# Seven quarter products in place of one: product 5 of the channel groups, with one buffer for x's two sets of combinations

## The reference, cut to what matters

```python
h = rmsnorm(x, norm_g)
proj = h @ w_in                       # 1024 -> 12288 channels
b_a, c_a, x_a, z_a, q, k, v, z_b, g_a, g_b = split(proj)
u = conv3(c_a * x_a) + conv_b         # causal, depthwise
y_a = (b_a * u * silu(z_a)) @ w_a_out
q, k = rotary(q), rotary(k)
o = retention(q, k, v)                # 4 heads, chunks of 128
y_b = (rms(o) * silu(z_b)) @ w_b_out
x = x + (sigmoid(g_a) * y_a + sigmoid(g_b) * y_b) @ w_o
out = rmsnorm(x, final_g)
```

## Time and profile before

| | |
|---|---|
| median of the runs | 1368.4 us |
| the profiled execution's span | 1366.5 us |
| around the span, by these two | 1.9 us |
| TensorE busy | 1354.6 us, 99% |
| VectorE busy | 1063.1 us, 78% |
| ScalarE busy | 591.4 us, 43% |
| GpSimd busy | 473.3 us, 35% |

### The profile page before, as it was taken

One profiled execution on the slowest core, in us unless ns is written; L12 is line 12 of the kernel. 1 busy time (PEld: TensorE's weight loads), 2 busy tenths in 40 slices (PEclk: granted clock), 3 DMA queues, 4 the chain that ended last, 5 costly groups with the idle time before them and its releaser, 6 DMA issues.

```text
span 1366.5 us, 16902 instructions
## 1 busy us (share of the span) xinstructions
PE 1354.6 (99%) x6498; PEld 1138.4 (83%) x6498; DVE 1063.1 (78%) x1053; ACT 591.4 (43%) x801; POOL 473.3 (35%) x349
## 2 busy tenths in 40 slices
PE   9999999999999999999999999999999999999997
PEld 7888888888888888888888888888888888888886
DVE  6898474578877777788888888747776998788887
ACT  7843233323222233234333333438778434433445
POOL 0100232244555554555555666415454001100002
PEclk9999999999999999999999999999999999999999
DMA  9746313322212222355443444657767699945443
GB/s 338 215 128 216 114 56 124 124 77 77 77 50 63 74 62 62 109 154 154 138 140 124 116 146 141 198 193 254 264 229 261 142 327 312 233 164 200 161 86 124
DMA packets 106128, 212.74 MB, mean 156 GB/s; under 512 B 6977, under 2 KB 49089, under 8 KB 101185
## 3 DMA queue, kind: packets, MB, share of 16 engines
q1 hardware_dynamic: 103024, 193.82, 42.4%
q0 software_dynamic: 2880, 17.83, 6.6%
q10 hardware_dynamic: 144, 0.02, 0.0%
HBM read 148.20 MB, written 55.05 MB: 149 GB/s over the span
## 4 chain that ended last, share of the span: by engine, by line
PE 95%; issue 1%; ACT 1%; DVE 1%; POOL 1%; DMA 0%; SPq 0%; POOLq 0%; DVEq 0%; ACTq 0%
PE psum L2488 16%; PE psum L2489 16%; PE psum L2486 16%; PE psum L2623 7%; PE psum L2625 7%; PE psum L2624 7%; PE psum L2413 4%; PE psum L2415 4%; PE psum L2416 4%; PE psum L2430 2%; PE psum L2432 2%; PE psum L2431 2%; PE psum L2531 2%; PE psum L2533 2%; PE psum L2532 2%
## 5 line engine op out<-in xcount | busy, mean ns | idle before, releaser
L2488 PE MATMUL psum<-hc,slots 128*128 128x512 f32 x976 | 379.8, 389 | 0.0
L2486 PE MATMUL psum<-hc,slots 128*128 128x512 f32 x976 | 379.8, 389 | 0.0
L2489 PE MATMUL psum<-hc,slots 128*128 128x512 f32 x976 | 379.8, 389 | 0.0
L1088 ACT ACTIVATE slots<-work 128x1024 fp32r<-128x1024 f32 (+1 forms) x158 | 162.0, 1036 | 435.9 <-PE psum L2489 329.0
L1583 DVE TENSOR_TENSOR slots<-work,slots 128x1024 fp32r<-128x1024 f32 (+1 forms) x158 | 228.6, 1448 | 39.0 <-ACT slots L1088 39.0
L2489 PEld LDWEIGHTS psum<-hc,slots 128*128 128x128 f32 x976 | 183.2, 188 | 38.1
L2486 PEld LDWEIGHTS psum<-hc,slots 128*128 128x128 f32 x976 | 183.2, 188 | 37.5
L2488 PEld LDWEIGHTS psum<-hc,slots 128*128 128x128 f32 x976 | 183.2, 188 | 37.3
L1348 ACT ACTIVATE last_slot<-arena 128x1024 fp32r<-128x1024 f32 x112 | 118.6, 1062 | 163.0 <-PE psum L2625 156.8
L2623 PE MATMUL psum<-last_slot 128*128 128x512 f32 (+1 forms) x452 | 175.3, 388 | 0.0
L2625 PE MATMUL psum<-last_slot 128*128 128x512 f32 (+1 forms) x452 | 175.0, 387 | 0.0
(11 more groups left out here) (214 smaller groups left out, 2331.2 us busy)
## 6 DMA issues: line engine op xcount, KB each, us to landing
work<-w_channel SPq DMA_DIRECT2D x80, 512.0 KB, 3.7
arena<-w_last SPq DMA_DIRECT2D x19, 1024.0 KB, 7.5
qk<-qk_scratch SPq DMA_DIRECT2D x32, 512.0 KB, 3.4
arena<-w_last POOLq DMA_DIRECT2D x9, 1024.0 KB, 11.4
v_raw<-value_scratch SPq DMA_DIRECT2D x32, 256.0 KB, 3.7
arena<-gate_scratch SPq DMA_DIRECT2D x16, 512.0 KB, 7.1
value_c<-w_value SPq DMA_DIRECT2D x10, 512.0 KB, 4.8
rows_of_x<-x_rows SPq DMA_DIRECT2D x8, 512.0 KB, 8.8
```

Source lines behind the costliest of these rows:

```text
L1088: nc.scalar.activation(slots[:, u % SLOTS, 0, 0:columns_of(u)], src, ACT.Copy).then_inc(w_hi, 1)
L2486: nc.tensor.matmul(bank, slot[:, 0, w], x_high, start=product in STARTS and j == 0, stop=False, skip_group_check=True)
L2488: nc.tensor.matmul(bank, slot[:, 0, w], x_low, start=False, stop=False, skip_group_check=True)
L2489: last = nc.tensor.matmul(bank, slot[:, 1, w], x_high, start=False, stop=j == 3, skip_group_check=True)
```

## The change

In groups 2 to 18 (`FIFTHS`) product 5 too becomes two units: three quarter products, then four. The new second half has p = 8 and stands between product 5's first half and product 7. Each such group has nine units.

```diff
+FIFTHS = range(2, GROUPS - 1)
+LAST_HALF, FIFTH_HALF = 7, 8
+UNIT_TABLE = [(g, p) for g in range(GROUPS) for p in (0, 1, 2, 3, FIFTH_HALF, 4, 5, 6, LAST_HALF)
+              if (p != FIFTH_HALF or g in FIFTHS) and (p != LAST_HALF or g in TWICE)]
...
+    return 3 * QUARTER if n == 6 and g in TWICE or n == 3 and g in FIFTHS else 2 * HALF
```

GpSimd makes the four sums for product 5 in its queue ahead of those for product 4:

```diff
             if turned:
                 silu(g - 1, 3)
+            if g in FIFTHS:
+                second_sums(g, 5)
             if g in TWICE:
-                second_sums(g)
+                second_sums(g, 4)
```

VectorE reads the shared bank, adds the rest, and adds the product. The work of the places stays where it was; only the splits follow the new table:

```diff
                 if n == 6 and g in TWICE:
-                    second_first(g)
-                elif n == 7:
-                    second_rest(g)
+                    second_first(g, 4)
+                elif n == LAST_HALF:
+                    second_rest(g, 4)
                     low(u + 1)
                     add(g, 4)
+                elif n == 3 and g in FIFTHS:
+                    second_first(g, 5)
+                elif n == FIFTH_HALF:
+                    second_rest(g, 5)
+                    add(g, 5)
                 elif ORDER[n] not in (1, 2):
                     add(g, ORDER[n])
```

TensorE's quarter products are the function of before, with the product as an argument. The waits for x's combinations are new:

```diff
+            loads = hx_loads(g, product) if g in FIFTHS else 0
...
             product_of_quarters(u, 1, quarter(2), c11)
+            if loads:
+                pe.wait_ge(t4_in, 16 + 16 * loads)
             product_of_quarters(u, 2, second("T4"), c21).then_inc(unit_done, 1)
             pe.wait_ge(w_ready, u + 2)
+            if loads:
+                pe.wait_ge(t1_t2_in, 16 + 16 * loads)
...
-            pe.wait_ge(value_sum, second_added(g, 1))
+            pe.wait_ge(value_sum, second_added(g, product, 1))
             product_of_quarters(u + 1, 0, second("T2"), one_six).then_inc(unit_done, 1)
```

`hx` (1.5 MB over the core) holds x's combinations of product 5 and of product 4 by turns. Both sets are kept in DRAM (`hx_d`); SyncE loads them twice in a group:

```diff
+        def load_hx(product):
+            n = int(product == 5)
+            sp.dma_start(hx[:, 2].bitcast(F32), hx_d[n, :, 2]).then_inc(t4_in, 16)
+            sp.dma_start(hx[:, 0:2].bitcast(F32), hx_d[n, :, 0:2]).then_inc(t1_t2_in, 16)
...
+            if g in FIFTHS and g > FIFTHS.start:
+                sp.wait_ge(unit_done, ended_at(g - 1) + 1)
+                load_hx(5)
...
-                sp.wait_ge(w_ready, unit_at(g, 5) + 1)
+                sp.wait_ge(w_ready, fifth_ended_at(g) + 1)
                 load_work(g + 1, "d", 3)
...
+            if g in FIFTHS:
+                sp.wait_ge(unit_done, fifth_ended_at(g) + 1)
+                if g == FIFTHS.start:
+                    sp.wait_ge(fifth_kept, 80)
+                load_hx(4)
             if g:
                 stores[kind_of(g - 1)](g - 1)
```

More of the change, by code:

```diff
@@ L108, in ended_at, with fifth_ended_at, product_at @@
     return unit_at(g, 4) + (g in TWICE)
+def fifth_ended_at(g):
+    return unit_at(g, 5) + (g in FIFTHS)
+def product_at(n):
+    return 5 if n == FIFTH_HALF else ORDER[min(n, 6)]
 def columns_of(u):
-    return 3 * QUARTER if u >= VALUE_UNITS and place_of(u)[0] in TWICE and place_of(u)[1] == 6 else 2 * HALF
+    if u < VALUE_UNITS:
+        return 2 * HALF
+    g, n = place_of(u)
+    return 3 * QUARTER if n == 6 and g in TWICE or n == 3 and g in FIFTHS else 2 * HALF
 def place_of(u):
@@ L121, in summed_until, with second_summed, second_added, hx_loads @@
 def summed_until(g):
[L123 to L133, removed]
+    return 16 + 4 * g + 4 * len([n for n in TWICE if n < g]) + 4 * len([n for n in FIFTHS if n < g])
+def second_summed(g, product, n):
+    return summed_until(g) + 4 + 4 * (product == 4 and g in FIFTHS) + n
+def second_added(g, product, n):
+    return 20 + 4 * (g - TWICE.start) + 4 * len([f for f in FIFTHS if f < g or f == g and product == 4]) + n
+def hx_loads(g, product):
+    return 2 * (g - FIFTHS.start) + (product == 4)
 def before(order, product):
@@ L1465, in _ @@
                 second_high("T3")
+            if g == FIFTHS.start and p == 1:
+                for name in ("T1", "T2", "T4", "T3"):
+                    fifth_high(name)
             if 0 < g <= GROUPS:
@@ L2018, in _ @@
                 second_low("T3")
+            if g == FIFTHS.start - 1 and p in (1, 2):
+                for n in range(2):
+                    t5_quarter(2 * (p - 1) + n)
+            if g == FIFTHS.start - 1 and p in (4, 5):
+                for name in (("T1", "T3"), ("T2", "T4"))[p - 4]:
+                    t_sum(name, t5_quarters, t5_sums, 20)
+            if g == FIFTHS.start and p == 2:
+                for name in ("T1", "T2", "T4", "T3"):
+                    fifth_low(name)
             if g == CONVS.start and p == 0:
@@ L2598, in _ @@
                     retention_begins(product)
-                if product == 4 and g in TWICE:
-                    second_units(g)
+                if product == 4 and g in TWICE or product == 5 and g in FIFTHS:
+                    second_units(g, product)
                 else:
```

148 lines of the change are left out of this document (93 added, 55 removed).

## The result

The changed kernel takes 1470.63 us (median of 4 runs, 1469.28 to 1471.96) against 1368.39 (1368.09 to 1368.44): 1.0746 times as long, 95% interval [1.0732, 1.076]. The forecast was 1470. Its profiled execution spans 1469.8 us against 1366.5.

What follows compares the result with a forecast made beforehand. TensorE, busy 99% of the span, was taken as the bound. Profile 1366.5 + 98 (the 8.5 us gain already off) + 4 for the clock = 1468.5, with 1.9 around it 1470 us; range 1425 to 1505.

Steps and rivals of the forecast that it cites:

- What goes: Product 5 on TensorE falls from 5.45 to 4.95 us in 17 groups, 8.5 us less in all.
- A conv group: Groups 3 to 9: chain through GpSimd, ScalarE and VectorE delays TensorE; group 42.7 us against 37.6, +5.1 each.
- The wait at product 4: Late in a conv group TensorE waits for VectorE's `second_first` for product 4: 2 us more.
- A turn group: Groups 12 to 18: TensorE waits 5.9 us for `second_first`; group about 45 us, +7.4 each.
- The sum: Group costs over groups 2 to 18 add to +98 us, the 8.5 us gain already taken off.
- The loads of hx: SyncE's 1.5 MB, twice a group, are hidden by 1 to 5 us; priced at nothing.
- Rival 3: Loads of hx land late beside a turn group's stores, 2 x 16 us on top, about 1500; 6%.
- `t5_quarter` and `t_sum` in group 1: Eight VectorE instructions of 512 columns, priced at nothing, at worst 5.5 us once.
- The clock: Part of product 7 may run at half clock in groups 11 to 18: 0 to 30 us, taken as 4.
- Turns on SBUF: VectorE and GpSimd alternate whole instructions on SBUF; without this lock the conv chain would be some 2 us shorter.
- Rival 1: The cover holds: no wait decides at product 5's shared-bank read, so the kernel gets faster, 1360; 8%.
- Rival 2: Only the first waits in conv and turn groups are paid, later ones caught up in products 7 and 3: 1436; 8%.

Runs made afterwards that it cites:

- experiment 5: Changed kernel with TensorE repeating one quarter product of product 5 eight times before its wait, in groups 11 to 18: 1465.25 us.
- Experiment 3: Changed kernel with VectorE's read of the shared bank for product 5 ahead of product 7's split and place 3's work: 1464.89 us.
- experiment 2: Changed kernel without GpSimd's four sums for product 5 and without ScalarE's wait for them: 1422.56 us.
- experiment 4: Changed kernel without SyncE's loads of hx and TensorE's waits for them: 1469.77 us.
- 12: Changed kernel without GpSimd's sums for product 5, its shared-bank reads cut to one column and the first read moved earlier: 1394.61 us.

## Why the forecast was right

**What goes** (8.5 us). Product 5 takes 4.95 us where it is not held, and is held in every group: so of the 8.5 nothing is seen by itself.

**A conv group.** Forecast and found, in us from the group's start at 362.27: sums' end 17.1 and 16.5; low part's end 19.4 and 18.9; `second_first` 24.0 and 23.6; split of 4's first half 29.5 and 29.3; s1 35.1 to 37.4 and 34.9 to 37.3; `second_first` for product 4 41.85 and 41.5; the group 42.7 and 42.4 (from the wait at 301.05 to that at 598.12, 297.07 us for 7 groups, 42.44 each). Two terms inside are off. The first wait is 0.34 us idle and some 0.5 in time (it ends at 381.24, where 380.74 was to be had), not 1.1: the taps held the sums for 378.78 - 374.40 - 2.94 = 1.44 us, not 1.8. (The forecast's own terms, 12.2 + 2.94 + 1.8, give 16.9 for the sums' end and not 17.1.) The wait at product 4, forecast as 2, is 1.8 us in three of the seven groups and 0.3 in three others; the last section shows that the clock makes the difference, and that it hardly changes the group's length.

**A turn group.** Sums 12.3 to 15.25, found 13.05 to 16.0; low part's end 17.5, found 18.4; the read's end 26.4, found 27.1; the wait 5.9, found 5.64 on average (45.1 us in 8). Everything is 0.7 to 0.9 later than forecast, because the group's start was taken from the first time round: s2 of the group before ends 660.47 + 2.40 - 659.55 = 3.3 us into the group and not 2.45, so that the splits of product 6 and, at 670.54, of product 5 stand 0.9 later in VectorE's queue. The forecast had this lateness (s2's end at 3.5), but carried only 0.3 us of it into the group's length. The group is 45.46 us (from the wait at 641.30 to that at 959.53, 7 groups), forecast 45; some 0.7 of it is the clock (experiment 5). The working put its +7.4 together as wait and lateness, said "It isn't the sum that decides but the order" (the sum of the added time is meant), and named the wait as the price of what stands in front of the read. Experiment 3 shows that this is the wrong reading of a right number: with 5 us of it out of the way 44.7 of 45.46 remain, and experiment 5 has the same 44.7 with the order as it was. GpSimd's four sums count for more: without them (experiment 2) the group is 41.1. The sum came out because it followed each engine's queue once around the group, not because of that wait.

**The sum.** By the starts of the groups, found and forecast: group 2 +1.6 and +1.4; groups 3 to 9 +34.6 and +36; group 10 +1.9 and +2.4; group 11 +7.2 and +6.5; groups 12 to 18 +57.4 and +52, to which most of the 4 us for the clock belong. With the 0.6 us by which group 2 starts late this is 103.3 us, forecast 98 + 4 = 102. No term is far off, so the total is not luck; that the small errors cancel to within 1 us is.

**What was priced at nothing.** The loads of hx: experiment 4, -0.9 us, less than the spread. Rival 3 is out. `t5_quarter` and `t_sum` in group 1: group 2 starts 0.6 us later than before (238.22 for 237.62), at worst 5.5 by the forecast.

**The clock.** Forecast 4 us net, measured 5.4 in groups 11 to 18 (experiment 5). Its place was forecast wrong: the granted clock was to be below 1.00 only in turn groups, since the waits of a conv group are shorter than the idle time at the kernel's end after which it fell, and it is 0.96 in four conv groups too (4, 6, 7 and 8). Groups 5 and 6, one at 1.00 and the next at 0.96:

```profile
362.30:404.70 42.40, 37.94 (x207) 32.65 (x206) 34.92 (x29) 11.41 (x13) 23.93 (x16) 1.00 0.41 137
404.70:447.10 42.40, 39.43 (x205) 33.62 (x204) 33.43 (x29) 11.41 (x13) 22.77 (x16) 0.96 0.42 136
```

**Turns on SBUF.** The added sums stretch from 0.73 to 1.18 and 1.72 us between the taps, `conv_product` from 0.68 to 2.86 beside s3. The forecast needed this, and the Trainium skill's rule (SBUF — State Buffer, section "Who interferes with whom") that one of the two engines holds the shared ports for its whole instruction agrees with these rows. The clock's rule (TensorE: Matmul & The Clock Gate, section "HAM oscillation — how this bites in real kernels") agrees in that TensorE restarts at half rate in each of the groups 11 to 18; that most of this is hidden here is what experiment 5 adds.

**Rival 1** (1360) is refuted by experiments 3 and 12: neither the earlier read nor the earlier read with the sums left out, so that none is waited for, covers the work. **Rival 2** (1436, only the first waits) is refuted by the 42.4 and 45.5 us a group repeated over all groups: nothing is caught up.

## What to carry over

When a matmul stream at 99% is made shorter by work on the engines that feed it, forecast by walking each feeding queue once around its period, with the turns on shared memory, and not by the first wait: the wait that the profile then names is where TensorE meets the longer loop, and moving the instructions in front of it gave back 6 us of 102. Once the stream is no longer the bound, work that had been free (here the silu products, 20 us) is paid for as well. Compare such runs group by group, with the clock beside: the reads gave 23 us in all with and without the sums, but from different groups. And a fallen clock costs what of its stretch falls on the loop: in the turn groups here the 0.6 us for which VectorE waited, of 2.6.

## Not expected of the hardware

Two conv groups of the changed kernel run the same instructions at different clocks. Behind the wait of 2.31 us that ends at 385.93 (TensorE's rows above) it stayed at 1.00 (the stretch is shown in the columns used above):

```profile
385.00:387.00 2.00, 1.07 (x8) 1.03 (x9) 2.00 (x4) 0.82 (x2) 0.00 (x0) 1.00 0.43 117
```

One group on, behind a wait of 2.30 us, it fell. The stretch behind that wait:

```profile
430.00:432.00 2.00, 2.00 (x6) 1.52 (x6) 1.83 (x4) 0.13 (x1) 0.00 (x0) 0.50 0.76 211
```

TensorE's two waits of that group, by its timeline:

```profile
428.27 0.39 PE L2522 MATMUL psum<-hx,slots 128*128 128x256 f32 x1 [2.30 <-DVE tp_first L1800]
...
446.33 0.39 PE L2522 MATMUL psum<-hx,slots 128*128 128x256 f32 x1 [0.32 <-DVE tp_v L1800]
```

Where the clock fell, the wait at product 4 is 0.32 us in place of 1.81, and the group hardly longer, 42.53 us for 42.34: nearly all of the slow stretch was taken off the next wait. In group 7, where it fell sooner, so that VectorE had to wait 0.59 us for the last quarter product, the group takes 43.21. The clock also fell behind a wait of 1.79 us (experiment 2, conv groups) and, in experiment 3, after two waits of 0.96 and 0.88 us that end 1.9 us apart (682.93 and 684.79; 0.69 in the 5 us from 685). Yet it stayed at 1.00 behind waits of 2.37 us in the groups 12 to 18 of experiment 2. So the length of a wait alone does not tell whether the clock falls; what else decides, these runs do not show.
